# Reordering the first output projection of a hybrid block: weights split within the scan, high products first

## The reference

```python
def finish(y, z, hy):
    y = rmsnorm(y.reshape(b, L, SSD_WIDTH) * jax.nn.silu(z), norm_g)
    g = hyena_op(hy, hy_conv_w, hy_conv_b, hy_filt, hy_bias)
    return jnp.concatenate([y, g], axis=-1) @ w_out     # w_out: 2048 x 1024
...
x = x + mod_l[2] * o_l
```

## Time and profile before

| | us |
|---|---|
| median of 3 runs | 2242.46 (2240.27 to 2247.51) |
| profiled execution, its own time | 2243.61 |
| its span in the trace | 2241.8 |
| TensorE busy | 2114.9 |
| VectorE, GpSimd, ScalarE busy | 857.2, 810.1, 441.2 |
| mean granted TensorE clock | 0.967 of full |

### The profile page before, as it was taken

One profiled execution on the slowest core, in us unless ns is written; L12 is line 12 of the kernel. 1 busy time (PEld: TensorE's weight loads), 2 busy tenths in 40 slices (PEclk: granted clock), 3 DMA queues, 4 the chain that ended last, 5 costly groups with the idle time before them and its releaser, 6 DMA issues.

```text
span 2241.8 us, 29888 instructions
## 1 busy us (share of the span) xinstructions
PE 2114.9 (94%) x11842; PEld 1684.1 (75%) x11842; DVE 857.2 (38%) x1245; ACT 441.2 (20%) x830; POOL 810.1 (36%) x438
## 2 busy tenths in 40 slices
PE   7989998999989978999999999999889999999997
PEld 2477656887877757878888888887676677888886
DVE  4533544212337674332212122233346663322334
ACT  3331110001345551031100001102116602100110
POOL 1443536112227765243223323224310034444443
PEclk9999999999989989999999999998989999999999
DMA  9444323333110011112111211111210022223222
GB/s 385 156 136 140 122 95 114 117 122 116 63 57 1 1 38 52 62 45 69 64 44 65 78 60 65 48 61 61 94 39 1 1 72 74 92 79 114 96 75 76
DMA packets 50791, 182.31 MB, mean 81 GB/s; under 512 B 5568, under 2 KB 6080, under 8 KB 49664
## 3 DMA queue, kind: packets, MB, share of 16 engines
q1 hardware_dynamic: 49600, 171.92, 22.4%
q10 hardware_dynamic: 576, 5.97, 0.7%
q0 software_dynamic: 512, 2.95, 0.4%
HBM read 178.72 MB, written 2.10 MB: 81 GB/s over the span
## 4 chain that ended last, share of the span: by engine, by line
PE 87%; DVE 5%; POOL 3%; DMA 2%; ACT 2%; issue 1%; DVEq 0%; SPq 0%; ACTq 0%
PE psum L516 21%; PE psum L521 21%; PE psum L517 21%; PE psum L1102 2%; PE psum L1090 2%; PE psum L1119 2%; DMA weights<-in_wall 2%; PE psum L583 1%; PE psum L703 1%; PE psum L739 1%; PE psum L918 1%; PE psum L943 1%; PE psum L545 1%; PE psum L666 1%; PE psum L539 1%
## 5 line engine op out<-in xcount | busy, mean ns | idle before, releaser
L2146 POOL TENSOR_TENSOR weights_lo<-weights,weights_hi 128x1024 fp32r<-128x1024 f32 (+1 forms) x228 | 505.1, 2216 | 1012.5 <-DVE weights_hi L1623 1012.5
L521 PE MATMUL psum<-normed_lo,weights_hi 128*128 128x512 f32 x1760 | 508.3, 352 | 0.0
L1623 DVE CAST weights_hi<-weights 128x1024 fp32r<-128x1024 f32 (+1 forms) x232 | 165.6, 715 | 885.5 <-PE psum L521 740.8
L516 PE MATMUL psum<-normed_hi,weights_hi 128*128 128x512 f32 x1088 | 391.5, 360 | 6.7 <-DVE weights_lo L1719 3.9
L517 PE MATMUL psum<-normed_hi,weights_lo 128*128 128x512 f32 x1088 | 373.9, 358 | 0.0
L521 PEld LDWEIGHTS psum<-normed_lo,weights_hi 128*128 128x128 f32 x1760 | 285.4, 190 | 16.5
L516 PEld LDWEIGHTS psum<-normed_hi,weights_hi 128*128 128x128 f32 x1088 | 204.7, 188 | 56.8 <-POOL weights_lo L2146 4.3
L516 PE MATMUL psum<-normed_first_hi,weights_hi 128*128 128x512 f32 (+1 forms) x672 | 233.8, 348 | 11.7 <-POOL weights_lo L2146 8.7
L517 PEld LDWEIGHTS psum<-normed_hi,weights_lo 128*128 128x128 f32 x1088 | 205.4, 189 | 34.9 <-issue 1.0
L517 PE MATMUL psum<-normed_first_hi,weights_lo 128*128 128x512 f32 (+1 forms) x672 | 214.9, 341 | 0.0
L516 PE MATMUL psum<-hidden_hi,weights_hi 128*128 128x512 f32 (+1 forms) x528 | 189.0, 358 | 0.0
(11 more groups left out here) (312 smaller groups left out, 2966.0 us busy)
## 6 DMA issues: line engine op xcount, KB each, us to landing
weights<-in_wall SPq DMA_DIRECT2D x264, 512.0 KB, 3.9
weights<-in_wall SPq DMA_DIRECT2D x32, 384.0 KB, 3.2
weights<-in_wall SPq DMA_DIRECT2D x32, 320.0 KB, 3.0
residual<-in_xT SPq DMA_DIRECT2D x1, 3072.0 KB, 17.3
residual<-in_xT ACTq DMA_DIRECT2D x1, 3072.0 KB, 11.0
phase<-in_tab ACTq DMA_DIRECT2D x2, 1280.0 KB, 5.5
normed<-in_window SPq DMA_DIRECT2D x1, 1536.0 KB, 12.6
normed<-in_window POOLq DMA_DIRECT2D x1, 1536.0 KB, 10.3
```

Source lines behind the costliest of these rows:

```text
L516: mm(acc[:, lo:hi], WH[:, b, k, :], high[:, lo:hi], start=st, stop=False)
L521: ins = mm(acc[:, lo:hi], WH[:, b, k, :], low[:, lo:hi], start=False, stop=en)
L1623: dve.tensor_copy(WH[:, b, 0:n, :], W[:, s, HALF * b:HALF * b + n, :]).then_inc(w_hi, 1)
L2146: TT(WL[:, s, at, :], W[:, s, at, :], WH[:, b, 0:width(gs[0], b), :].bitcast(f32), ALU.subtract).then_inc(w_lo, 1)
```

## The change

The diff has five parts. (1) A second home for high weights, WHX, is laid over the last 2048 columns of the residual; G0 and G0+2 use it (`high_home`). VectorE casts G0's halves and GpSimd subtracts them behind the scan's turns 0 and 1 (`between`), after steps 1 and 3. (2) The residual's last three tiles, which WHX covers, are loaded by SP once G0+2 is done (`x2_in`), behind the loads of G0+5. (3) TensorE runs all high products of G0 first, then its low ones tile by tile, with G0+1's Hyena half between and behind them. (4) The gated halves run together: the high products of all three, then their low products by tile, so that the three blocks finish together. (5) The casts and subtractions of G0+1 to G0+3 are placed anew in VectorE's and GpSimd's order.

```diff
+        WHX = part("weights_first_hi", x_at, 4096, 2, HALF, P)
+        high_home = lambda g: WHX if g in (G0, G0 + 2) else WH
...
-        def chunk_turns(eng, body, unrolled=False):
+        def chunk_turns(eng, body, unrolled=False, between=None):
             body(0, (None, 4, 5, 5), False)
+            if between:
+                between(0)
             body(2, (5, 5, 4, 0), False)
+            if between:
+                between(1)
...
+                if at == G0 + 6:
+                    sp.wait_ge(blocks_done, 2 * G0 + 6)
+                    sp.dma_start(X[:, 5:KT, :], A["xT"][:, 5:KT, :]).then_inc(x2_in, 16)
-            cuts = {0, SLOTS, 4, 6, 8, G0 + 1, G0 + SLOTS, len(JOBS)}
+            cuts = {0, SLOTS, 4, 6, 8, G0 + 1, G0 + SLOTS, G0 + 6, len(JOBS)}
...
-            def between_tiles(k, blocks):
-                if k == 5 and blocks == (0, 1):
+            def high_products(g, b, u, k, start):
+                s = g % SLOTS
+                high, _ = mixed(k)
+                for lo, hi in SEGS:
+                    mm(pair(u)[:, lo:hi], high_home(g)[:, b, k % KT, :], high[:, lo:hi], start=start, stop=False)
+                    mm(pair(u)[:, lo:hi], WL[:, s, HALF * b + k % KT, :], high[:, lo:hi], start=False, stop=False)
+            def low_products(g, b, u, k, stop):
+                _, low = mixed(k)
+                for lo, hi in SEGS:
+                    ins = mm(pair(u)[:, lo:hi], high_home(g)[:, b, k % KT, :], low[:, lo:hi], start=False, stop=stop)
+                if k % KT == KT - 1:
+                    ins.then_inc(blocks_done, 1)
+            for b in range(2):
+                half_ready([G0], 0, b)
+                pair_ready([G0], 0, b)
+            for k in range(KT):
+                mixed_waits[0](k)
+                for b in range(2):
+                    high_products(G0, b, b, k, k == 0)
+            for k in range(KT):
+                mixed_waits[1](k)
+                for b in range(2):
+                    low_products(G0, b, b, k, False)
+                if k == 3:
+                    pe.wait_ge(yz_added, KT)
                     pe.wait_ge(yz_sums, 1)
                     token_sums(6).then_inc(yz_summed, 1)
-                if k == 7 and blocks == (0,):
+                    half_ready([G0 + 1], 0, 0)
+                    pair_ready([G0 + 1], 0, 0)
+                if k == 4:
                     pe.wait_ge(yz_rec, 1)
                     token_spread(6).then_inc(yz_spread, 1)
-            both_by_tile([G0], 0, mixed, SEGS, mixed_waits, between_tiles, False)
...
-            for g, b, u in ((G0 + 1, 1, 0), (G0 + 2, 0, 1), (G0 + 2, 1, 2)):
+                for h in ((), (), (), (0, 1), (2, 3), (4, 5), (6,), (7,))[k]:
+                    high_products(G0 + 1, 0, 2, h, h == 0)
+            for k in range(KT):
+                low_products(G0 + 1, 0, 2, k, False)
+            gated_parts = ((G0 + 1, 1, 0), (G0 + 2, 0, 1), (G0 + 2, 1, 2))
+            for g, b, u in gated_parts:
                 half_ready([g], 0, b)
-                tiles([g], pair(u), b, KT, gated, SEGS, False, True, gated_waits if u == 0 else None)
+                for k in range(KT):
+                    if u == 0:
+                        mixed_waits[0](KT + k)
+                    high_products(g, b, u, KT + k, False)
+            for k in range(KT):
+                mixed_waits[1](KT + k)
+                for g, b, u in gated_parts:
+                    low_products(g, b, u, KT + k, k == KT - 1)
...
-            act.dma_start(X[:, :, :], A["xT"]).then_inc(x_in, 16)
+            act.dma_start(X[:, 0:5, :], A["xT"][:, 0:5, :]).then_inc(x_in, 16)
...
-            chunk_turns(dve, turn)
+            chunk_turns(dve, turn, between=lambda b: split_high([G0], 0, b))
...
-            for b in range(2):
-                split_high([G0], 0, b)
             for k in range(KT):
+                if k == 5:
+                    split_high([G0 + 1], 0, 0)
                 TT(XBC[:, k, :], XBC[:, k, :], Z[:, k, :], ALU.mult).then_inc(yz_ready, 1)
...
             dve.memset(MARK[:, 0:1], 0.0).then_inc(yz_sums, 1)
+            split_high([G0 + 1], 0, 1)
             dve.wait_ge(n_sqrt, 2)
...
                 STT(XBC[:, k, :], XBC[:, k, :], vec("sng", k), NP, ALU.mult, ALU.mult).then_inc(n_mul, 1)
-                if k in (2, 4):
-                    next_high([G0], 0, k // 2 - 1)
+                if k in (3, 5):
+                    b = k // 2 - 1
+                    dve.wait_ge(blocks_done, 2 * G0 + 1 + b)
+                    split_high([G0 + 2], 0, b)
...
-                    next_high([G0 + 1], 0, 0)
-                    next_high([G0 + 1], 0, 1)
+                    dve.wait_ge(blocks_done, 2 * G0 + 3)
+                    split_high([G0 + 3], 0, 0)
                     for k in range(3):
+                        dve.wait_ge(blocks_done, 2 * G0 + 4 + k)
+                        if k == 0:
+                            split_high([G0 + 3], 0, 1)
                         residual(X[:, k, :], k, k)
...
-                        if k < 2:
-                            next_high([G0 + 2], 0, k)
...
+                        if name == "out0" and isinstance(r, int) and r == 2:
+                            dve.wait_ge(x2_in, 16)
...
-            chunk_turns(pool, turn)
-            low([G0], 0)
+            chunk_turns(pool, turn, between=lambda b: low([G0], 0, (b,)))
+            low([G0 + 1], 0, (0,))
             pool.wait_ge(yz_ready, KT)
             for n in range(2 * KT):
...
-                if n in (KT + 2, KT + 4):
-                    low([G0 + 1], 0, (n // 2 - 5,))
-            for g in (G0 + 1, G0 + 2):
-                low([g + 1], 0)
+                if n == KT - 1:
+                    low([G0 + 1], 0, (1,))
+                if n in (KT + 1, KT + 3):
+                    low([G0 + 2], 0, ((n - KT) // 2,))
+            low([G0 + 3], 0)
```

More of the change, by code:

```diff
@@ L339, in build_kernel @@
         a_ch, v_ch, g_ch = sem("act_order"), sem("dve_order"), sem("pool_order")
-        x_in, c_in, v_in, small_in, t3_in, t4_in, win_in, rope_in = (
-            sem(n) for n in ("x_in", "c_in", "v_in", "small_in", "t3_in", "t4_in", "win_in", "rope_in"))
+        x_in, x2_in, c_in, v_in, small_in, t3_in, t4_in, win_in, rope_in = (
+            sem(n) for n in ("x_in", "x2_in", "c_in", "v_in", "small_in", "t3_in", "t4_in", "win_in", "rope_in"))
         silu_c, mods_a, mods_b = sem("silu_c_ready"), sem("mods_a_ready"), sem("mods_b_ready")
@@ L1000, in between_tiles @@
                     pe.wait_ge(yz_rec, 1)
                     token_spread(6).then_inc(yz_spread, 1)
-            both_by_tile([G0], 0, mixed, SEGS, mixed_waits, between_tiles, False)
[L1004 to L1008, removed]
-            for g, b, u in ((G0 + 1, 1, 0), (G0 + 2, 0, 1), (G0 + 2, 1, 2)):
-                half_ready([g], 0, b)
-                tiles([g], pair(u), b, KT, gated, SEGS, False, True, gated_waits if u == 0 else None)
+                for h in ((), (), (), (0, 1), (2, 3), (4, 5), (6,), (7,))[k]:
+                    high_products(G0 + 1, 0, 2, h, h == 0)
@@ L1622, in split_high @@
                 dve.wait_ge(w_loaded[s][b], along([16 * (g // SLOTS + 1) for g in gs], i))
-                dve.tensor_copy(WH[:, b, 0:n, :], W[:, s, HALF * b:HALF * b + n, :]).then_inc(w_hi, 1)
+                dve.tensor_copy(high_home(gs[0])[:, b, 0:n, :], W[:, s, HALF * b:HALF * b + n, :]).then_inc(w_hi, 1)
             for c in range(2):
@@ L2145, in low @@
                     pool.wait_ge(w_hi, along([2 * NTH[g] + b + 1 for g in gs], i))
-                    TT(WL[:, s, at, :], W[:, s, at, :], WH[:, b, 0:width(gs[0], b), :].bitcast(f32),
+                    TT(WL[:, s, at, :], W[:, s, at, :], high_home(gs[0])[:, b, 0:width(gs[0], b), :].bitcast(f32),
                        ALU.subtract).then_inc(w_lo, 1)
```

## The result

The changed kernel took 2230.25 us (median of 5 runs, 2226.41 to 2231.49) against 2243.22 for the kernel before; the ratio is 0.9934 with a 95% interval of 0.9919 to 0.9949. That is 0.66% faster, and 1.2 us above the 2229.1 that were forecast.

A forecast was written before the change was run, and what follows sets the result against it. TensorE, busy 94% of the span, was taken as the bound, with gains only where it idles or runs at low clock. -21.4 + 4.8 + 1.2 + 2.0 = -13.4 us gave 2229.1 us, range 2222 to 2237.

The forecast's parts named there:

- scan, two insertions: In the scan: G0's casts and subtractions put into two steps cost 2.4 us each, +4.8 us, bounds 0 and 7.2.
- scan's end to the gated end, without the clock's term: From the scan's last heads to the end of the gated halves: TensorE's waits shrink, -21.4 us.
- the clock behind the sparse stretch: Dense TensorE work after 833.7 may start at 1.2 GHz: +2.0 us, bounds 0 and 2.75.
- wait in front of out0b: First matmul of out0b: TensorE newly waits for VectorE's residual 0, +1.2 us.
- Rival 1: In the scan: splits almost free, below 1 us each; total -17 to -20 us, about 2224; chance 16%.
- The four waits: In G0's low products: TensorE waits for hyena_lo tiles four times, about 1.1 us each.
- The third wait of before: TensorE's 8.52 us wait in the old kernel, put down to low weights of G0+1's second half.
- Rival 2: Behind the scan: clock stays at 1.2 GHz some 20 us from 826, costing up to 10 us; 2237; chance 9%.
- rival 3: In the scan: worse engine turns, 2.3 us more in each of ten remaining steps; +9.6 us, 2252; chance 6%.
- rival 4: In G0: high products wait anyway for psum pairs or mixed tiles; -5 to 0 us; within the remaining 7%.
- the first wait of 7.56 us: TensorE's wait behind the scan for G0's low weights in the old kernel; forecast to vanish.

The follow-up runs named there:

- gated_in_turn: Changed kernel with the gated halves one after the other, high and low products of each tile together; ratio 0.9968 to the kernel before.
- undo_scan_split: Changed kernel with both splits of G0 (casts and subtractions) back behind the scan, all else kept; ratio 0.9941 to the kernel before.
- cast_only_in_scan: Changed kernel with only VectorE's two casts of G0 in the scan, GpSimd's two subtractions behind it; ratio 0.9927 to the kernel before.
- cast_only_hold: Casts-only-in-scan kernel with GpSimd's subtractions also held until VectorE's last weighing of the scan is done; ratio 0.9924 to the kernel before.
- lows_by_block: Changed kernel with the low products of the three gated halves block by block instead of tile by tile; ratio 0.9935 to the kernel before.

## Why the prediction was right

| term | forecast | measured |
|---|---|---|
| scan, two insertions | +4.8 | +4.4 |
| scan's end to the gated end, without the clock's term | -21.4 | -20.3 together |
| the clock behind the sparse stretch | +2.0 | (0.30 x 5.6 = 1.7 of it) |
| wait in front of out0b | +1.2 | +1.1 |
| sum | -13.4 | -14.7 (-14.4 between the marks of the table above); medians -13.0 |

- **How close, and why.** That the time lies 1.2 us from the forecast is in part luck. The same kernel's five times reach from 2226.41 to 2231.49 us, and the stretches gained 14.4 us where 13.4 were forecast. Without the clock's 1.7 the part from the scan's end to the gated end gained some 22.0 us, for 21.4.
- **The scan.** The mechanism was right: GpSimd's queue from the first to the second add_carried has no slack, and GpSimd there was late enough for the exponential to wait 3.85 us. 2.4 for each insertion was a little much; 2.67 and 2.29, with 0.5 given back. The split of the price was right too: most of it is the subtraction. Rival 1 (almost free) fell for this place and came nearly true for another (1.0 us for both).
- **G0.** TensorE began without a wait and stayed at 1.00. hyena_lo started 10.7 us behind the last heads, 10.5 being forecast, but by another way: I let one product wait for GpSimd's subtraction (1.9 us) and the subtraction run free. In the trace the three products took 2.68 us and the subtraction 4.78. The sum was the same, because hyena_lo waits for both. The four waits were shorter than the 1.1 us forecast for each (some 0.82 us for three of them, 3.6 together), but each burst took 0.96 us for 0.70, so the pace was hyena_lo's 1.78 us all the same. The normalising products started 25.3 us behind the scan, for 23.9 forecast, with the clock's 1.7 us in front of them.
- **The third wait of before** was misread: the prediction puts it down to G0+1's second half. The job's first half, the Hyena half of block 2, is what TensorE waited for; the matmuls right behind the wait read hyena_lo. The wait's length and its cause (the subtraction stands behind three ssd_lo tiles) are right, and the sum doesn't change.
- **The gated halves.** No wait in them, and gated_in_turn shows what running them together spares: 4.9 us.
- **The clock.** It did fall, for a cost of 1.7 us in this trace. What was not seen: where in the sparse stretch it falls decides whether it costs anything. Rival 2 fell: dense work raised it again within 5.6 us.
- **The rivals left.** The scan's period stayed at 12.50 us (rival 3), and the high products waited for nothing (rival 4).
- **What the prediction did not say** is how the parts share the gain. It charged the first wait of 7.56 us to the splits in the scan as their yield. undo_scan_split shows that with the new order this yield is 4.2 to 4.5 us, since hyena_lo then sets the pace of the low products and TensorE would have caught up; that is the price paid in the scan. Put into the idle gap, both splits pay: 303.2 us for scan and behind, against 306.5 in undo_scan_split. With the casts alone in the scan it is 305.0 us, in two traces.

Not settled: whether the two falls of the clock ahead of the scan have a common cause. They differ between traces of the same kernel.

## What to carry to other kernels

Work moved into a loop that is bound by a chain costs what the place costs: behind the instruction whose engine goes on without a gap it was 2.2 us each, in the same step's idle gap 0.5 us. Look at which instruction ends the idle time, and put the work in front of it. Early weights brought nothing while the product order stopped at the next late input; first take the products whose inputs are all there, and split off the late ones. When blocks are made to end together, finish one of them early, so that its read-out lies under the others.

## What was unexpected of the hardware

- VectorE and GpSimd held each other up, but which one waited varied: beside G0's subtractions products took up to 3.1 us for 0.94; in the changed kernel three products ran at full pace and the subtraction took 4.78 us for 2.41.
- In cast_only_in_scan a GpSimd operation that started 0.14 us ahead of a VectorE operation on the chain made it take 2.77 us for 0.69 and the scan end 2.5 us later; held back behind it, in cast_only_hold, it didn't.
- After TensorE had gone over to bursts of four matmuls every 1.8 us, its clock fell from 1.00 (2.4 GHz) to 0.50 (1.2 GHz) some 3 us later in the trace of lows_by_block, still in the sparse stretch, and some 9 us later in that of the changed kernel, in the dense work behind it. The token sums start 18.74 us behind the scan's end in both; the fall cost nothing up to there in the first, and 1.7 us of dense work in the second.
